# Expert rows of a PEER layer: slots of 32 tokens by four heads in place of 128 tokens of one head, on one core

## The reference

```python
q = (xb @ wq).reshape(PEER_BLOCK, PEER_HEADS, PEER_QDIM)      # 8 heads of 256
s1 = einsum('thd,nd->thn', q[..., :half], keys1)              # 128 keys each
s2 = einsum('thd,nd->thn', q[..., half:], keys2)
v1, i1 = top_k(s1, 16); v2, i2 = top_k(s2, 16)
cand = v1[..., :, None] + v2[..., None, :]                    # 256 sums
top_s, top_i = top_k(cand, 16); gate = softmax(top_s)         # 16 experts
act = gelu(einsum('td,thkd->thk', xb, u[expert]))
out = einsum('thk,thkd->td', gate * act, v[expert])
```

## Time and profile before

| | us |
|---|---|
| median of 3 runs | 1842.85 |
| lowest, highest | 1841.39, 1857.53 |
| span of the profiled execution | 1846.5 |
| PE, DVE, ACT, POOL busy in it | 1473.6, 1090.8, 458.5, 804.3 |

### The profile page before, as it was taken

The page is one execution under the profiler, slowest core; times in us unless marked ns, Lnnn a source line. Parts: engine busy times, 40 slices in busy tenths (PEclk is TensorE's granted clock), DMA queues, the critical chain, the costliest instruction groups (busy, mean ns, idle before and its releaser), DMA issues.

```text
span 1846.5 us, 20807 instructions
## 1 busy us (share of the span) xinstructions
PE 1473.6 (80%) x7541; PEld 699.2 (38%) x7541; DVE 1090.8 (59%) x2812; ACT 458.5 (25%) x1105; POOL 804.3 (44%) x776
## 2 busy tenths in 40 slices
PE   8989989878999767869889988778779865666665
PEld 7544566336733222433347433233433321111111
DVE  3413278137678475682487693774952699855554
ACT  1121323102210433332122114343330232211111
POOL 0000000005542376672465331675643467777773
PEclk9999878989999987889999999898979997666666
DMA  8985346759999999998999999899989999999996
GB/s 279 329 264 167 113 145 180 239 183 377 408 409 409 350 349 395 359 358 338 394 406 408 409 409 375 285 409 379 327 297 392 373 366 380 394 397 410 409 409 265
DMA packets 212949, 625.16 MB, mean 339 GB/s; under 512 B 17748, under 2 KB 55828, under 8 KB 212664
## 3 DMA queue, kind: packets, MB, share of 16 engines
q0 software_dynamic: 110736, 402.88, 56.7%
q1 hardware_dynamic: 102112, 220.96, 33.1%
HBM read 611.55 MB, written 12.23 MB: 338 GB/s over the span
## 4 chain that ended last, share of the span: by engine, by line
PE 45%; DMA 16%; DVE 16%; POOL 13%; issue 6%; ACT 4%; SPq 1%; DVEq 0%; ACTq 0%
PE bank L658 16%; POOL BIG L551 13%; PE bank L631 8%; PE bank L588 8%; DMA BIG<-in_peer_v_dram,BIG 7%; DMA BIG<-in_peer_u_dram,BIG 6%; PE bank L724 5%; DVE BIG L1405 4%; DMA wbuf<-in_w_in_dram 4%; PE bank L698 3%; ACT BIG L1073 2%; DVE BIG L1648 1%; DVE BIG L1676 1%; PE bank L953 1%; PE bank L638 1%
## 5 line engine op out<-in xcount | busy, mean ns | idle before, releaser
L551 POOL DMA_INDIRECT BIG<-in_peer_u_dram,BIG x384 | 402.6, 1049 | 588.5 <-DVEq L1803 430.0
L588 PE MATMUL bank<-BIG 64*64 64x512 f32 x3072 | 483.9, 747 | 211.2 <-DMA BIG<-in_peer_v_dram,BIG 129.0
L551 POOL DMA_INDIRECT BIG<-in_peer_v_dram,BIG x384 | 398.8, 1038 | 429.0 <-PE bank L588 341.7
L1405 DVE CUSTOM_DVE_ANT_0 BIG<-BIG 128x1024 f32<-128x1024 f32 x384 | 462.1, 1224 | 185.5 <-DMA BIG<-in_peer_u_dram,BIG 182.5
L658 PE MATMUL bank<-wbuf,BIG 128*128 128x512 f32 x832 | 385.0, 617 | 12.9 <-DMA wbuf<-in_w_in_dram 6.2
L588 PEld LDWEIGHTS bank<-BIG 64*64 64x64 f32 x3072 | 113.5, 155 | 536.3 <-issue 337.0
L658 PEld LDWEIGHTS bank<-wbuf,BIG 128*128 128x128 f32 x832 | 158.8, 196 | 234.4 <-issue 208.1
L1073 ACT ACTIVATE BIG<-bank 128x512 f32<-128x512 f32 (+5 forms) x231 | 117.7, 539 | 463.2 <-PE bank L698 144.5
L1073 ACT ACTIVATE BIG<-cst,small 128x64 f32<-128x64 f32 x384 | 112.0, 339 | 403.1 <-DVE small L1400 401.4
L631 PE MATMUL bank<-wbuf,BIG 128*128 128x512 f32 x320 | 150.7, 627 | 8.7 <-DMA wbuf<-in_w_in_dram 8.2
L1073 ACT ACTIVATE small<-small 128x2 f32<-128x2 f32 (+1 forms) x204 | 41.5, 205 | 420.6 <-DVE small L1405 409.8
(11 more groups left out here) (163 smaller groups left out, 1046.4 us busy)
## 6 DMA issues: line engine op xcount, KB each, us to landing
wbuf<-in_w_in_dram SPq DMA_DIRECT2D x108, 1024.0 KB, 11.2
wbuf<-in_w_ssm_br_dram SPq DMA_DIRECT2D x24, 1024.0 KB, 7.4
wbuf<-in_peer_wq_dram SPq DMA_DIRECT2D x24, 1024.0 KB, 8.9
wbuf<-in_w_attn_br_dram SPq DMA_DIRECT2D x12, 1024.0 KB, 7.2
wbuf<-in_w_out_dram SPq DMA_DIRECT2D x12, 1024.0 KB, 7.8
BIG<-in_state_ssm_dram SPq DMA_DIRECT2D x16, 512.0 KB, 6.2
out_s_ssm_dram<-BIG SPq DMA_DIRECT2D x16, 512.0 KB, 3.8
BIG<-in_peer_u_dram,BIG POOLq DMA_INDIRECT x384
```

The costliest lines, as they stand in the source:

```text
L551: pool.indirect_dma_start(slot, None, table, bass.IndirectOffsetOnAxis(ap=eidx[:, col:col + 1], axis=0)).then_inc(done, 16)
L588: last = mm(acc[i][64 * half:64 * half + 64, :], dg[rows, :], vslot[k][rows, 512 * half:512 * half + 512], start=False, stop=False, skip_g ...
L1405: nc.vector.tensor_tensor_reduce(uslot[s], uslot[s], H[k // BLOCKS], 1.0, 0.0, ALU.mult, ALU.add, dots[k % 2][:, j:j + 1]).then_inc(dot_do ...
```

## The change

A slot now holds 32 tokens of four heads: partition p is token 32 s + p % 32 and head p / 32 (of a half of the heads), where s is one of four groups of tokens. The slots of a block are two groups, `2 * pair` and `2 * pair + 1`. A diagonal is then 128 rows by 32 columns (`fan`, four identities of 32 under each other), and the rows of v are summed over the four heads within one product of 128 rows into 32 columns, two products for a slot in place of four. The dots need `h` laid out in the same way, so PE copies each group of 32 tokens to all four quarters of the partitions (`fan_out`, 8 products of 32 rows, 512 columns), and ACT brings them to `fanned`, which all the ticks of the tile read in place of `H`. There is one `fanned`, so ACT first waits for the last dot of the tile before. The scores come by halves of wq (two products, four heads): for each pair of token groups a bank, written by 16 products of 32 columns for 32 tokens and one head. `pick` is the same code; its parts are now half 0 with groups 0 and 1, half 0 with groups 2 and 3, and so on. Number and size of the gathers, dots and ticks stay. The room comes from masks that are now built by DVE from one table of 128 columns, from two tiles' `gate` and `eidx` for three, and from `H` of the last tile in `stateT`.

```diff
+def place_of(b, j):
+    part, k = b % BLOCKS // PART, b % PART
+    return b // BLOCKS % 2 * P + 32 * part + PTOP * j + k, part % 2 * 2 + j
 ...
-                        gather(table_u, uslot[k], WB * b + j, u_in[k])
+                        gather(table_u, uslot[k], place_of(b, j)[0], u_in[k])
 ...
                 dg = diag[:, b % DIAGS * WB + j, :]
-                for i in range(2):
-                    rows = slice(64 * i, 64 * i + 64)
-                    for half in range(2):
-                        last = mm(acc[i][64 * half:64 * half + 64, :], dg[rows, :],
-                                  vslot[k][rows, 512 * half:512 * half + 512], start=False, stop=False, skip_group_check=True)
+                pair, odd = divmod(place_of(b, j)[1], 2)
+                for half in range(2):
+                    at = 64 * half + Q * odd
+                    last = mm(acc[pair][at:at + Q, :], dg, vslot[k][:, 512 * half:512 * half + 512],
+                              start=False, stop=False, skip_group_check=True)
 ...
+                def fan_out():
+                    for s in range(4):
+                        rows = slice(Q * s, Q * s + Q)
+                        for half in range(2):
+                            dst = sbank()
+                            sf.give(mm(dst[:, :], fan[rows, :], H[q.n][rows, 512 * half:512 * half + 512],
+                                       start=True, stop=True))
                 phase("wq")
-                for j in range(2):
-                    product(xT, sf, sbank)
-                    steps.at("wq")
-                    scores((j,), vf, vbank)
+                product(xT, sf, sbank)
+                steps.at("wq")
+                product(xT, sf, sbank)
+                scores(0, vf, vbank)
+                steps.at("wq")
                 for j in range(2):
                     steps.at("late")
                     product(xT, sf, sbank)
                 steps.at("late")
                 steps.limit = q.n * BLOCKS + PART
-                scores((2, 3), sf, sbank)
+                fan_out()
+                scores(1, sf, sbank)
 ...
                 for j in range(2, 4):
                     steps.at("late")
                     keep_qp(j)
-                exp_scores(q.n, 0)
                 steps.at("late")
                 steps.limit = q.n * BLOCKS + PART
+                if q.n:
+                    act.wait_ge(dot_done, WB * BLOCKS * q.n)
+                for s in range(4):
+                    for half in range(2):
+                        src = bank()
+                        sd.give(f(fanned[:, s, 512 * half:512 * half + 512], src[:, :]))
                 keep_qT((2, 3))
                 for quarter in (2, 3):
                     src = bank()
                     sd.give(f(sc[:, quarter * 512:(quarter + 1) * 512], src[:, :]))
+                exp_scores(q.n, 0)
 ...
                 if k < TOTAL:
+                    if k % BLOCKS == 0:
+                        dve.wait_ge(sb_drained, SR + before[k // BLOCKS, "wq"][1] + 14)
                     for j in range(WB):
                         s = k % RING * WB + j
                         dve.wait_ge(u_in[s], 16 * (k // RING + 1))
-                        nc.vector.tensor_tensor_reduce(uslot[s], uslot[s], H[k // BLOCKS], 1.0, 0.0, ALU.mult,
+                        nc.vector.tensor_tensor_reduce(uslot[s], uslot[s], fanned[:, place_of(k, j)[1], :], 1.0, 0.0, ALU.mult,
                                                        ALU.add, dots[k % 2][:, j:j + 1]).then_inc(dot_done, 1)
```

More of the change, by code:

```diff
@@ L74, in const_table @@
     parts["same"] = np.stack([np.ones((P, P)), same], 1)
-    adm = np.zeros((P, TILES, 2 * P))
-    for tile in range(2):
-        q = (tile * P + t) // CHUNK
-        k = np.arange(2 * P) // CHUNK
-        adm[:, tile] = k[None, :] <= q[:, None]
-    adm[:, 2, :P] = 1
-    adm[:, 2, P:] = same
-    parts["adm"] = adm
-    parts["nadm"] = (1 - adm) * NEG
+    parts["chunks"] = (t // CHUNK)[None, :] <= (t // CHUNK)[:, None]
     parts["blk"] = stream[:, None] == np.arange(DEC_B)[None, :]
     odd = stream % 2
-    parts["id64"] = (t % 64)[:, None] == np.arange(64)[None, :]
+    parts["fan"] = (t % Q)[:, None] == (t % Q)[None, :]
     parts["par"] = odd[:, None] == np.arange(2)[None, :]
@@ L1086, in tick @@
                     for j in range(WB):
[L1087 removed]
+                        last = f(diag[:, (k - 1) % DIAGS * WB + j, :], fan[:, 0:Q], scale=w8[(k - 1) % 2][:, j:j + 1])
                     last.then_inc(diag_ready, 1)
@@ L1305, in mixer @@
                 act.wait_ge(h_ready, q.n + 1)
-                for j in range(2):
-                    keep_qp(j)
-                    steps.at("wq")
-                    keep_qT((j,))
+                keep_qp(0)
+                steps.at("wq")
+                keep_qp(1)
+                keep_qT((0, 1))
+                steps.at("wq")
                 for j in range(2, 4):
@@ L1550, in index_scores @@
                                 own.settle()
-                    own(tt(s, s, adm[:, t, 0:S], ALU.mult))
+                    mask, late, away = chunks if t < 2 else same[:, 1, :], s[:, S - P:S], q.scoret[:, 0:P]
+                    own(tsc(away, mask, -NEG, NEG, ALU.mult, ALU.add))
+                    own(tt(late, late, mask, ALU.mult))
                     own.settle()
-                    own(tt(s, s, nadm[:, t, 0:S], ALU.add))
+                    own(tt(late, late, away, ALU.add))
                     own.settle()
```

57 lines of the change are left out of this document (31 added, 26 removed).

## The result

The changed kernel takes **1886.27 us** (median, 1884.76 to 1891.86), the kernel before 1843.78 us (median of four runs): 1.0215 times as long, interval 1.0169 to 1.0261. The forecast was 1857 with 1830 to 1877, so the change costs three times what I gave it. The profiled execution has a span of 1884.4 us, 37.9 above that of before.

What follows compares the result with a forecast made beforehand. DMA was taken as full in most stages once gathers run, with 49 us idle in two attention stretches. 30 us lost and 16 gained put the 1846.5 span at 1860.5; less 3.65 for the median, 1857 us, range 1830 to 1877.

Steps and rivals of the forecast that it cites:

- The next tile's weights fill DMA: four buffers of 1 MB are 10 us. I take 8: After the second tile: the wait chain stands, but weights cover 10 us of it; loss 8 us, 0 to 19.
- The weights and ten gathers cover 23 us; I take 4: After the first tile: gathers begin 6.5 us later, fan-out adds 7.5 to PE, mostly covered; loss 4 us, 2 to 10.
- The chain behind the fan-out in the last tile: Last tile: later indices, fan-out and copies delay the exp and pause POOL's gathers; loss 5 + 10 + 3 = 18 us.
- PE has filled two banks, the other six products at 0.88: Last tile's fan-out: after the dots at 1493, six products remain at 0.88 us each, copies done at 1500.
- The gain of 14: Halved v products in the two stretches with idle DMA: 14 us gained, with 0 and 28 as ends.
- I expect that in the last stretch alone: Blocks whose two slots land apart, still taking two waves, were expected only in the last stretch, at no cost.
- well under half of 484: Sign of being right: the new v products' line L589 busy well under half of 484 us.
- Slower, about 1876: Rival: PE's clock falls further in the two stretches with room; gain 5, losses 38, about 1876 us; chance 0.18.
- Losses covered: Rival: the waits cost only their lower ends (13, 3 and 2) against a larger gain; about 1838 us; chance 0.24.
- The groups don't overlap: Rival: a v block stays at 1.8 us or more, nothing gained, 30 lost; about 1872 us; chance 0.06.
- Faster: Rival: PE sets the stages with room, 40 of 49 us idle DMA return, losses 17; about 1820 us; chance 0.14.
- The other signs to watch: Two DMA holes of some 10 us after ten gathers, DVE's exp wait 12 us or more, last tile's gather 5 later.

Runs made afterwards that it cites:

- after: The changed kernel as first profiled, against the kernel before: 1886.27 us, 1.0215.
- after_again: The changed kernel unaltered, run and profiled a second time: 1.0223 of the kernel before.
- b_exp: The kernel before with only ACT's exp of part 0 moved behind the last tick and the second half's four copies, no fan-out: 1.0089.
- b_late: The kernel before with only the search's first scores moved behind the second product of wq: 1.0060.
- a_exp: The changed kernel with ACT's exp of part 0 back ahead of the tick with the old tile's last gelu: 1.0076 of the kernel before.
- a_nofan: The changed kernel with the exp ahead of that tick and no fan-out, dots reading H directly (wrong tokens): 0.9965 of the kernel before.
- a_early: The changed kernel with the exp ahead of the tick and the first and last tiles' fan-out right behind the first scores: 1.0067 of the kernel before.
- a_split: a_early with the second tile's fan-out also in two halves, around the tick: 1.0084 of the kernel before.
- b_cols: The kernel before with only the v products in their new form, 128 rows into 32 columns (sums mix tokens): 0.9928, and 0.9882 on another chip.
- b_delay: The kernel before with, in the second tile alone, the exp behind the tick, the second half's copies and 26 dummy ACT copies: 1.0121.
- a_tok3: The changed kernel, wq's first half by 64 tokens, first and last tiles' fan-out halved behind late ticks, exp ahead of the fourth product's copy: 1.0026 of the kernel before.

## Why the prediction was wrong

By its own steps, with S1 to S3 of after and after_again:

- **"The next tile's weights fill DMA: four buffers of 1 MB are 10 us. I take 8": the largest error.** S2 is +13.9 and +14.2 with the products' gain in it (3.1 to 6.3), so the loss is 17 to 20 us. The failed step is the cover. PE frees the buffers by its next convolution products, which stand behind the same ticks: SP stood 39.7 us for L725, and no weight moved from 958 to 985. Only pauses of about 5 us vanished (b_exp, b_late).
- **"The weights and ten gathers cover 23 us; I take 4": the same error after the first tile.** S1 is +8.2 and +4.5 with a gain of 5.6 in it, a loss of 10 to 14 us. In after the weights' queue moved nothing from 425 to 450, SP stood up to 32.1 us for L725 (16.6 before), and POOL stood 8.23 us for its eleventh gather (1.69 before). The search was 7.2 us late, where 6.5 was expected. The size is the least certain: a_exp and a_nofan have -2.3 and -2.1, so 7 to 10 us go with the exp's place (13.8 us late), but S1 is good to 5 us only, and a_early and a_split, with an exp 10.3 late, have +1.3 and +8.0 from the same code.
- **The chain behind the fan-out in the last tile: right in its links, short in size.** "DVE stands 18 to 24 us later": 23.7 later against the start of S3. "It then stands for 11 to 16 us less 2.5 ... I take 10": POOL stood 8.25 + 4.68 = 12.9. Indices +5: they came +5.3. The sum was taken at 18, with 13 to 22, and S3 is +22.6 and +25.3, at and above the top; 5.3 + 12.9 are 18.2 of it, and the rest of 4 to 7 stands where 3 were put for DVE. The link that was mis-sized is the fan-out's products: "PE has filled two banks, the other six products at 0.88" is 5.3 us after the dots, and the row at 1508.14 has all eight in 10.21 us, 1.28 each. The reason for half the clock was also another one. The prediction had it from PE standing idle for 10 us; the granted clock (PEclk, the third number from the end) fell within the fan-out, with PE busy all the time:

```profile
1495.00:1508.00 13.00, 13.00 (x42) 4.79 (x40) 12.26 (x34) 1.85 (x7) 1.81 (x2) 1.00 0.38 142
1508.00:1511.00 3.00, 3.00 (x11) 1.15 (x8) 0.49 (x2) 1.67 (x5) 2.08 (x4) 1.00 0.84 268
1512.00:1518.00 6.00, 6.00 (x9) 1.92 (x8) 0.00 (x0) 2.39 (x4) 4.60 (x5) 0.50 1.00 375
```

- **The gain of 14: in its range, 9 to 22 by what one takes.** 9 us in S1 and S2 of b_cols, 13 and 22 by the ratios. How it comes was sized wrongly: I had the products' busy time halved, and L589 has 65.0 and 69.3 us in the stretches of the earlier trace rows, where L588 had 89.0 and 94.8, a fall of 27%:

```profile
590.00:850.00 260.00, 64.99 (x288) 8.70 (x288) 0.79 0.96 361
1110.00:1440.00 330.00, 69.34 (x328) 8.88 (x328) 0.81 0.95 358
```

  Where a block's two slots land together it takes 1.07 us for eight records against 1.95. Where DMA delivers them apart, each has its own (PE's timeline of after):

```profile
495.71 1.05 PE L589 MATMUL bank<-BIG 128*32 128x512 f32 x4 [1.14 <-DMA BIG<-in_peer_v_dram,BIG]
...
520.67 1.07 PE L589 MATMUL bank<-BIG 128*32 128x512 f32 x8
```

  Four records take as long as eight, so a split block takes 2.10 us for 2.18 before and saves next to nothing. "I expect that in the last stretch alone" was wrong; three of the eight blocks between 480 and 560 are split. The other part is the clock: from 1110 to 1440 there are 37 rows of x8, of which 16 take 1.06 or 1.07 us and 14 take 1.85 to 1.94, as one does at 634.09, with 0.50 granted from 634 to 636. L589 is busy 365.4 us in all, where "well under half of 484" was a sign of being right.
- **The rivals.** "Slower, about 1876" was nearest in time, but not by its mechanism: it was to decide from a clock under 0.75 in 590 to 850. It was 0.79, and 0.78 in b_cols, which is faster than before. Its clock fell, though less, and its losses of 38 came mostly from the waits. The Trainium skill (TensorE: Matmul & The Clock Gate, the two states), by which an idle PE goes back to 1.2 GHz, is borne out: the row 960 to 970 of b_delay has PE idle at 0.50. In the last tile the measurement goes further: there the clock fell while PE was busy (the rows above). "Losses covered" failed with the weights. "The groups don't overlap" fell with the row of 1.07: by the rule of the Trainium skill (TensorE: Matmul & The Clock Gate, The mechanism) that LDWEIGHTS overlaps running products only when the row group differs, the prediction had 1.8 for it, so the row does not bear the rule out here. "Faster" would have needed 40 us of DMA time; S1 and S2 of b_cols got 9.
- **The other signs to watch** were there: the hole in DMA's share behind the tenth gather, the wait for the exp, the first gather 5 us late. From that gather (1505.88) to the end are 378.5 us, where 374 was expected.

Told as terms, S1 to S3 are 24 + 18.5 + 12 = 54.5 us lost and 9 gained, where I had 30 and 16 (no separate test, since the losses are the stretches with the gain added). The stretches themselves are +44.7 and +44.0; S0 was 6 to 7 us short, as it can be without any cause in the code, which makes the +38 of the span.

## What to carry to other kernels

Work that is small in sum can still be dear where it stands: eight products and twelve copies put between a search's indices and its exp cost 17 of 23 us in the last stretch, and most of the change's cost went when they were moved, with nothing removed. When a transfer-bound kernel pauses its own issue, do not count the next weights as cover before asking who frees their buffers: here it was an engine that stood in the same pause. Count the gathers already issued (here some 5 us) and take a long pause at its full length. After moving a wait, look at the next instruction of the same in-order engine: here it was a new wait each time.

## What the runs showed of the hardware

- A PE that is busy by the profile can still be granted half the clock. In the last tile of after PE is busy without a gap from 1495 to 1518, and the clock is 1.00 up to 1511 and 0.50 from 1512, within the fan-out's products of 32 rows; why, no run here tests. In the second tile, between 960 and 970, PE is busy 8.62 of 10 us, mostly with such products, at 0.50. Six of them took 9.29 us, 1.55 each, against 0.88 for a 128-row product at the full clock; the two ahead of a wait of 2.59 us took 0.99 each.

```profile
951.85 1.98 PE L1041 MATMUL bank<-BIG,cst 32*128 32x512 f32 x4
956.42 9.29 PE L1041 MATMUL bank<-BIG,cst 32*128 32x512 f32 x12 [2.59 <-ACT BIG L1088]
```

- Products of 128 rows into 32 columns each overlap by column groups: at the full clock four (eight records) take 1.06 to 1.07 us, and two take 1.05. The saving is there only if both slots are present.
- S0, in which no gather runs, differs by up to 12 us between profiles of these kernels (373.4 in a_split, 385.3 in a_tok3), more than most effects looked for here.
